# Input projection in the order of its waiters, and layer 1's modulation between the expert slots of two sample blocks

## The reference

```python
m = silu(cond) @ w_ada + b_ada                  # w_ada (1024, 6144): the modulation, for c_ctx and for c
sh1, sc1, g1, sh2, sc2, g2 = split(m, 6)
h = rmsnorm(x, norm1_g) * (1 + sc1) + sh1
proj = h @ w_in                                 # c_q, c_kv, k_pe | z | xbc | dt | glu
mix = concat(attention, ssd(z, xbc, dt), conv_module(glu)) @ w_out
x = x + g1 * mix
h = rmsnorm(x, norm2_g) * (1 + sc2) + sh2
q = h @ peer_wq                                 # 8 heads, top 16 of 128 x 128 keys: 128 experts a token
x = x + g2 * sum_k gate_k * gelu(u[idx_k] . h) * v[idx_k]
```

## Time and profile before

| | |
|---|---|
| median of 3 runs | 5076.69 us (5076.66 to 5082.86) |
| profiled execution | 5067.13 us |
| its span | 5065.3 us, mean TensorE clock 0.918 |
| PE, DVE, ACT, POOL busy | 3905.9, 3247.4, 743.5, 1442.1 us |
| gathers (software queue) | 1342.26 MB, 66.2% of 16 engines |
| direct loads | 153.13 MB, 9.4% |

### The profile page before, as it was taken

One profiled execution on the slowest core, in us unless ns is written; L12 is line 12 of the kernel. 1 busy time (PEld: TensorE's weight loads), 2 busy tenths in 40 slices (PEclk: granted clock), 3 DMA queues, 4 the chain that ended last, 5 costly groups with the idle time before them and its releaser, 6 DMA issues. The chain is left out here.

```text
span 5065.3 us, 36421 instructions
## 1 busy us (share of the span) xinstructions
PE 3905.9 (77%) x11046; PEld 1925.4 (38%) x11046; DVE 3247.4 (64%) x8263; ACT 743.5 (15%) x2205; POOL 1442.1 (28%) x1284
## 2 busy tenths in 40 slices
PE   7479577889777777778868776789987777777776
PEld 6365233554223222235535632346432322222222
DVE  1534866644887867854474648664468787687666
ACT  0121124311101001010022111341111100100101
POOL 0001122211444444432222011222134444344432
PEclk9689688999998999999989887899999999999999
DMA  8244346763998998999959334567469999899998
GB/s 262 71 131 142 140 174 225 260 220 128 404 418 362 421 421 365 421 395 390 371 205 355 135 125 159 205 237 259 156 252 421 388 401 421 366 421 421 415 421 343
DMA packets 342149, 1497.72 MB, mean 296 GB/s; under 512 B 31424, under 2 KB 176448, under 8 KB 178112
## 3 DMA queue, kind: packets, MB, share of 16 engines
q0 software_dynamic: 184320, 1342.26, 66.2%
q1 hardware_dynamic: 157632, 153.13, 9.4%
HBM read 1491.97 MB, written 3.31 MB: 295 GB/s over the span
## 5 line engine op out<-in xcount | busy, mean ns | idle before, releaser
L650 PE MATMUL expert_acc<-uv_ring,diag 128*128 128x512 f32 x3744 | 1895.4, 640 | 430.1 <-DVE diag L1207 420.7
L604 POOL DMA_INDIRECT uv_ring<-uv,expert_index x936 | 1051.9, 1124 | 2816.8 <-PE expert_acc L650 2249.1
L650 PEld LDWEIGHTS expert_acc<-uv_ring,diag 128*128 128x128 f32 x3744 | 702.1, 201 | 1515.1 <-DVE diag L1207 898.2
L1198 DVE CUSTOM_DVE_ANT_0 uv_ring<-uv_ring,arena 128x1024 f32<-128x1024 f32 x680 | 832.0, 1224 | 236.9 <-DMA uv_ring<-uv,expert_index 234.1
L650 PE MATMUL expert_acc<-arena,diag 128*128 128x512 f32 x1376 | 692.4, 636 | 258.1 <-DVE diag L1207 189.8
L1207 DVE TENSOR_SCALAR diag<-const_mats,expert_gate,gelu 128x128 f32<-128x128 f32 x1280 | 465.4, 364 | 372.9 <-ACT gelu L929 276.4
L929 ACT ACTIVATE gelu<-u_dot 128x1 f32<-128x1 f32 x1280 | 256.3, 203 | 2995.9 <-DVE u_dot L1198 2991.9
L604 POOL DMA_INDIRECT arena<-uv,expert_index x344 | 390.0, 1134 | 763.6 <-PE expert_acc L650 465.2
L1198 DVE CUSTOM_DVE_ANT_0 arena<-arena 128x1024 f32<-128x1024 f32 x344 | 420.9, 1224 | 174.1 <-DMA arena<-uv,expert_index 172.4
L650 PEld LDWEIGHTS expert_acc<-arena,diag 128*128 128x128 f32 x1376 | 248.6, 197 | 692.9 <-DVE diag L1207 403.4
L1198 DVE CUSTOM_DVE_ANT_0 uv_ring<-uv_ring,prompt_rows 128x1024 f32<-128x1024 f32 x256 | 312.2, 1220 | 86.8 <-DMA uv_ring<-uv,expert_index 86.1
(11 more groups left out here) (201 smaller groups left out, 2788.3 us busy)
## 6 DMA issues: line engine op xcount, KB each, us to landing
w_ring<-w_ada SPq DMA_DIRECT2D x66, 512.0 KB
w_ring<-w_in SPq DMA_DIRECT2D x64, 512.0 KB
w_ring<-w_pq SPq DMA_DIRECT2D x64, 512.0 KB
w_ring<-w_out SPq DMA_DIRECT2D x32, 512.0 KB
uv_ring<-w_ada SPq DMA_DIRECT2D x30, 512.0 KB, 6.0
uv_ring<-uv,expert_index POOLq DMA_INDIRECT x936
arena<-b_ada SPq DMA_DIRECT2D x48, 128.0 KB
arena<-uv,expert_index POOLq DMA_INDIRECT x344
```

Source lines behind the costliest of these rows:

```text
L604: pool.indirect_dma_start(out=UV[j], out_offset=None, in_=uv, in_offset=bass.IndirectOffsetOnAxis(ap=idxs[:, n % 2, k:k + 1], axis=0)).the ...
L650: ins = pe.matmul(acc[:, half, :], diag[:, m % DIAGS, :], UV[SLOT_AT[m]][:, D + 512 * half:D + 512 * half + 512], start=(k == 0), stop=(k ...
L1198: V_.tensor_tensor_reduce(UV[j][:, 0:D], UV[j][:, 0:D], rows_of(n), 1.0, 0.0, ALU.mult, ALU.add, dots[:, m % DOTS:m % DOTS + 1]).then_inc( ...
```

## The change

1. **Input projection.** px comes directly behind pa, each xt as soon as its silu can be there, then pg, and pz last: four tiles ahead of the taps on PE (two on ACT), the rest between the taps; DVE makes a gate of z after every third tap. On PE cs and cb now stand behind the taps' points, and DVE makes gm behind the taps. Units of w_in are loaded in the new order. The same in all four mixers.
2. **Modulation.** b_ada comes by one DMA as 24 rows of 256; a ninth product of each unit adds the row (a column of the identity, spread, times the rows). ACT drains the tiles instead of DVE. Layer 0's runs at the start as before, with the three layer-weight loads now behind its weights; ACT norms the prompt behind it.
3. **Layer 1's modulation** stands in the slots of sample blocks 2 and 3 of layer 0 (b = 1 and 2): one unit behind `add_v` and `gelu` of slots 5, 15, ..., 115, through `w_ring` alone. Silu(cond) is made at the start of block 2.
4. **Block 4** runs beside the prompt mixer alone; `BESIDE_PROMPT` has 138 advances for the 131 that a block needs, 52 of them ahead of the taps.
5. Small things: the product in `add_peer` is written in place in PSUM, iota and some scratch tiles are moved.

```diff
+def mod_unit_at(l, b, k):
+    return (b - 1) * ADA_UNITS // 2 + k // 10 if l + 1 < L and b in (1, 2) and k % 10 == 5 and k < 5 * ADA_UNITS else None

-BESIDE_PROMPT = points(("mod", range(24), 2), ("n1", [1], 3), ("pa", range(2), 2), ("pz", range(2), 2), ("px", range(6), 1),
-                       ("pg", range(4), 1), ("conv", [5], 2), ("taps", range(4, 30, 5), 1), ("cT", [0], 2), ("st", range(2), 3),
-                       ("yT", [0], 2), ("v", [0], 2), ("head", range(6), 2), ("wo", range(4), 2), ("n2", [1], 3),
-                       ("pq", range(16), 1))
+BESIDE_PROMPT = points(("n1", [1], 8), ("pa", range(2), 5), ("pz", range(2), 3), ("px", range(6), 3), ("pg", range(4), 3),
+                       ("conv", [5], 4), ("taps", range(4, 30, 5), 3), ("cT", [0], 4), ("st", range(2), 5), ("yT", [0], 4),
+                       ("v", [0], 4), ("head", range(6), 2), ("wo", range(4), 2), ("n2", [1], 4), ("pq", range(16), 1))

+def in_tiles(g):
+    nb = GROUP_BLOCKS[g]
+    return ([("pa", i) for i in range(2 * nb)]
+            + [("px", 0), ("px", 1), ("px", 2), ("xt", 0), ("px", 3), ("xt", 1), ("px", 4), ("xt", 2), ("px", 5), ("xt", 3),
+               ("pg", 0), ("xt", 4), ("pg", 1), ("pg", 2), ("pg", 3)])
+def with_taps(g, ahead):
+    n = 2 * GROUP_BLOCKS[g]
+    out = [("pz", i) for i in range(min(ahead, n))]
+    for k in range(CMK):
+        if k % 3 == 2 and ahead + k // 3 < n:
+            out.append(("pz", ahead + k // 3))
+        out.append(("taps", k))
+    return out
+POINTS_AT = {("xt", 0): [("px", 0)], ("xt", 1): [("px", 1)], ("xt", 2): [("px", 2)], ("xt", 3): [("px", 3)], ("xt", 4): [("px", 4)],
+             ("pg", 1): [("px", 5), ("pg", 0)], ("pg", 2): [("pg", 1)], ("pg", 3): [("pg", 2), ("pg", 3), ("conv", 5)]}
...
 # sync
+                sp.dma_start(bada[0:ADA_UNITS, :], b_ada[l].rearrange("(u n) -> u n", n=WU)).then_inc(s_brow.sem, 16)
+                for u in range(ADA_UNITS):
+                    load_w(w_unit(l, 0, "ada", u), w_ada[l, :, u * WU:(u + 1) * WU])
...
 # tensor: a unit (MOD_GROUPS[u]: unit u's product, then the transposes of the row before it)
+                        for c in range(DC):
+                            pe.matmul(t[:, 0:WU], hT[:, c, 0:P], w[:, c, :], start=(c == 0), stop=False)
+                        ins = pe.matmul(t[:, 0:WU], C[0:ADA_UNITS, C_ID, u:u + 1].broadcast_to([ADA_UNITS, P]), bada[0:ADA_UNITS, :],
+                                        start=False, stop=True)
...
                         for k in range(SLOTS):
                             add_v(n, k)
+                            unit = mod_unit_at(l, b, k)
+                            if unit is not None:
+                                modulate(l + 1, unit)
...
 # scalar
                             gelu(n, k)
+                            unit = mod_unit_at(l, b, k)
+                            if unit is not None:
+                                modulate(l + 1, unit)
...
+                        if (s, i) == ("px", 1) or s == "xt":
+                            silu_tanh(0 if s == "px" else i + 1)
+                            beside.point("px", 0 if s == "px" else i + 1)
...
 # vector
+                            if k % 3 == 2 and k // 3 < 2 * nb:
+                                gate_z(k // 3)
                             beside.point("taps", k)
```

More of the change, by code:

```diff
@@ L209, in psum_order @@
     for l in range(L):
-        out += [(s, l, 0, i) for s, i, _ in mod_steps()]
+        if l == 0:
+            out += [(s, 0, 0, i) for s, i, _ in itertools.chain(*MOD_GROUPS)]
         for g in range(2):
@@ L686, in _ @@
                     pe.wait_ge(*free["n1"].at(l, g, 2 * nb - 1))
[L687 to L717, removed]
+                    for s, i in in_tiles(g) + with_taps(g, 4):
+                        if s == "taps":
+                            beside.point("taps", i)
+                            continue
+                        if s == "xt":
+                            pe.wait_ge(*s_silu.at(l, g, i))
+                            t = fill("xt", l, g, i)
+                            src = ctmp[i % 2] if i < 4 else BC[:, 0]
+                            for b in range(nb):
+                                ins = turn(t[:, b * P:(b + 1) * P], src[:, b * P:(b + 1) * P])
+                        else:
+                            u = in_unit(s, i, nb)
+                            w = weights(l, g, "in", u)
+                            t = fill(s, l, g, i)
+                            if s in ("px", "pg"):
+                                for c in range(DC):
+                                    ins = pe.matmul(t[:, 0:T], w[:, c, (i % 2) * P:(i % 2 + 1) * P], hT[:, c, 0:T],
+                                                    start=(c == 0), stop=(c == DC - 1))
+                            else:
+                                b, width = i % nb, WU if u != 1 else TOK - 256
+                                for c in range(DC):
+                                    ins = pe.matmul(t[:, 0:width], hT[:, c, b * P:(b + 1) * P], w[:, c, 0:width],
+                                                    start=(c == 0), stop=(c == DC - 1))
+                        done(ins, s)
+                        for stage, k in POINTS_AT.get((s, i), [(s, i)] if s in ("pa", "pz") else []):
+                            beside.point(stage, k)
@@ L730, in _ @@
                                        start=True, stop=True), "cb")
-                    for k in range(CMK):
-                        beside.point("taps", k)
                     pe.wait_ge(*s_glu.at(l, g))
@@ L1314, in _ @@
                             ins.then_inc(s_cconv.sem, 1)
-                        for s, i in {0: [("px", i) for i in range(3)], 1: [("px", i) for i in range(3, 6)] + [("pg", i) for i in range(4)]}.get(c, []):
-                            beside.point(s, i)
                         if c >= 1:
```

276 lines of the change are left out of this document (142 added, 134 removed).

## The result

The changed kernel takes 5043.24 us (median of 4 runs, 5030.11 to 5048.69) against 5078.03 (4 runs, 5076.66 to 5082.86) beside it on the same chip: ratio 0.9927, 95% interval 0.991 to 0.9943. In a second session it was 5038.76 (5037.54 to 5047.22), ratio 0.9926 (0.9907 to 0.9945). So it is faster, by 0.7%. I had forecast 4945, and 5020 as the top of the range.

A forecast was written before the change was run, and what follows sets the result against it. DMA was taken to bound expert blocks and layer 1's modulation, PE and DVE order the sample mixers; −3 − 20 − 32 + 70 − 115 − 32 = −132 gave 4935 profiled, 4945 us median, 8-in-10 range 4885 to 5020.

The forecast's parts named there:

- Start, −3: Layer 0's modulation at the start: DVE's b_ada hole goes, −11.9, bias products add +10.9; sum −3 us.
- Prompt mixer of layer 0, −20: Layer 0's prompt mixer: z tiles leave the front, transposes and conv run between x tiles; −20 us.
- Sample mixers, −32 each: Both layers' sample mixers: taps start at 504.5 against 553.8, less z gates and later masks; −32 us each.
- the bill behind the last tap: Sample mixers: cs and cb queue behind the last tap's slots, so DVE waits for masks and ct; +13.4 us.
- Blocks 2 and 3, +70: Layer 0's sample blocks with the modulation units: +60 for DMA bytes, +5 a block for engine stops; +70 us.
- Layer 1's prompt mixer, −115: Stage from block 3's end, block 4 beside it: DMA-bound at 2.53 us a transfer, 446 us against 562; −115.
- The rule on ACT's tables: Conv steps: alternating tanh and gelu load a table each change; 2.66 us by the skill page would add some 11 us.
- Rival C: Whole kernel: forecast with the dearer table change, total −121, 4956 us; chance 0.04.
- D: Layer 1's prompt mixer: five-buffer ring sets a slower slot pace, 4.49 us or more; +8 to +73; chances 0.05 and 0.08.
- A: Blocks 2 and 3: the units' stops are not absorbed, blocks +163, total −39, 5038 us; chance 0.13.
- B: Layer 1's prompt mixer packs better through idle PE, stage about 400 us, total −178, 4899 us; chance 0.12.

The follow-up runs named there:

- e17: The changed kernel again, unedited, in the second session: 5038.76 us, ratio 0.9926.
- e2: Changed kernel with PE's slots of each conv chunk put ahead of its wait for the silu and the xt transposition: 4999.14 us, ratio 0.9851.
- e28: Changed kernel with e2's edit and one slot a point, not three, beside conv chunks and gate tiles of layer 1's prompt mixer: 4997.01 us, ratio 0.9841.
- e11: Changed kernel with all 128 slots of block 4 ahead of layer 1's prompt mixer, none beside it: 5058.34 us, ratio 0.9973.
- e15: Changed kernel with one slot a point beside the conv chunks, ring of four not five, four modulation units loaded ahead not five: 5227.26 us, one run.

## Why the prediction was wrong, step by step

*Start, −3.* Measured +0.8 (first pa tile 137.46, now 138.28). The hole behind the second unit is gone, as these rows of PE show, but the bias product costs more than I took:

```profile
25.72 0.69 PE L708 MATMUL rotating<-b_ada_rows,const_mats 24*128 24x256 f32 x2
26.34 3.72 PE L707 MATMUL rotating<-w_ring,hT 128*128 128x256 f32 x16
29.99 0.69 PE L708 MATMUL rotating<-b_ada_rows,const_mats 24*128 24x256 f32 x2
```

0.69 us for two, where I had 0.45 from sixteen in a run.

*Prompt mixer of layer 0, −20.* Measured −19 (sample transposes from 344.6 to 326.3, with the start's +0.8). *Sample mixers, −32 each.* Measured −30 and −24 (in e17's profile the second is −37). Taps at 485.8 (I had 504.5 less the 23 us of the earlier steps, 481.5), and the bill behind the last tap came as forecast:

```profile
554.62 0.76 DVE L1415 TENSOR_TENSOR arena<-rotating,const_mats 128x256 f32<-128x256 f32 x2 [4.13 <-PE rotating L769]
557.61 0.76 DVE L1415 TENSOR_TENSOR arena<-rotating,const_mats 128x256 f32<-128x256 f32 x2 [2.23 <-PE rotating L769]
```

*Blocks 2 and 3, +70.* Measured +69.4, DMA share 1.01. The number was right, its make-up only half: I added 60 for bytes and 10 for stops, and the runs show two limits, each near the whole cost by itself (+69 for the bytes, +53 for the stops), so that the sum came out is in part luck.

*Layer 1's prompt mixer, −115: the step that failed.* Measured −16.4 (567.6 to 551.2). In the words of the step: "52 + 9 units, less 3 prefetched units and 4 or 5 prefetched slots, is 54 × 2.53 = 137". With the 12 us before them that put the taps 149 us behind block 3; they came at 228.0, 79 us late. The other 20 us that are missing lie behind the first tap: the taps took 75 us, not 62, and from ct to yT it was 71.5, not 62.

Of the 79 us, 43 are the lock step, which the prediction didn't have: with e2's edit the taps come at 184.6. The other 36 are the price of a slot. 2.53 us was from a row with 21 slots and 9 weight units in 76.4 us, two queues side by side, and I called that row DMA-bound. Its stretch in the trace of before:

```profile
2464.00:2541.00 77.00, 71.20 (x313) 45.64 (x311) 38.23 (x89) 8.34 (x37) 20.99 (x20) 0.98 0.93 349
```

PE is busy 71 of 77 us there, as full as DMA at 0.93. Counted in slots alone the row says 3.64 us, and 12 + 47.5 × 3.64 = 185 is what e2 shows. This agreement is with one run and no law: e28, with 20 slots fewer there, needs 122.4 where the same price gives 112. Alone in the ring of five a slot took 2.84 us (e11), and with one buffer fewer and the same bytes the stage grew by 80 (e15), so the ring counts, not the bytes alone. Even with e2's edit the stage's DMA share is 0.81. How the 36, and the 20 behind the first tap, are shared between the ring and the mixer's own chain I didn't pull apart.

*The steps together.* +0.8 − 19 − 30 + 69.4 − 16.4 − 24 = −19, and the spans of the two profiles differ by 18.4.

*The rule on ACT's tables* fell with its premise. I wrote that tanh and gelu in turn load a table at each change. ACT's timeline of after, in the conv chunk and at dt's exponential behind it:

```profile
2369.75 0.20 ACT L970 ACTIVATE gelu<-u_dot 128x1 f32<-128x1 f32 x1 [3.10 <-DVE u_dot L1269]
2369.86 0.26 ACT L1050 ACTIVATE arena<-rotating 128x128 f32<-128x128 f32 x1
2372.55 0.28 ACT L1052 ACTIVATE arena<-rotating 128x128 f32<-128x128 f32 x1 [2.44 <-PE rotating L669]
2372.73 0.30 ACT L1031 ACTIVATE arena<-arena 128x128 f32<-128x128 f32 x1
...
2498.93 1.28 ACT L1042 ACT_TABLE_LOAD   x1
2500.22 0.21 ACT L1042 ACTIVATE dt<-dt 128x16 f32<-128x16 f32 x1
```

Between the gelu and the tanh (L1031) there is no load, nor any from 2350 to 2498; the whole kernel has 154 against 148 before. In all of it no load stands between a gelu and the next tanh (30 places), and none between a tanh and the next gelu in 29 of 37; in the other 8 an exponential or a logarithm had come just before the tanh. So loads go with exponentials and logarithms: at them, or at what follows. A load is 1.28 us, and in 99 of the 154 the function follows within 20 ns. So the drain of 1.38 us that the Trainium skill, ScalarE: Activation LUTs, What ACT_TABLE_LOAD costs, adds doesn't show here. The sum isn't touched: I had costed these loads at nothing. Rival C falls with the rule.

*The rivals.* D named the failing step: "a burst of 8 or 10 slots outruns" the ring, and "every further slot waits a full round". It had the bursts at the wrong place: the points of three beside the conv chunks did it, as PE's slots stood behind a wait for DVE. I gave D 0.13 together, priced at 4.49 us a slot and more; block 4 came to 508.4 / 128 = 3.97. Its argument against, that the modulation kept 377 GB/s with the same five buffers, held for slots with weight loads between them, which don't use the ring. A (blocks +163) and B (a better packed mixer) are refuted by the table. That A's total, 5038, lies 5 us from the measured median is chance: its blocks cost 69 and not 163, and the mixer's missing 99 us make up for that.

## What to carry to other kernels

Price work that goes through a ring by its own count in the nearest rows, never by all transfers of that stretch: other queues' bytes ride along and make the pace look better than the ring can give. Before work is moved out of a stretch, see whether its engines were full there (DMA 1.03, PE 171 of 172): then it was cover for what stays, and in another full stretch it can cost more (here 75.6 us, not 50.5). When two engines' slots are tied to points of another chain, put the slots that free buffers ahead of any wait for the engine that waits for those buffers.

## What the runs showed of the hardware

In the lock step TensorE's granted clock was 0.80 in the mean of 2341 to 2470, so part of the stretch at the lower of its levels, 1.2 GHz and not 2.4, and it was busy 0.59 of it. In e2's stretch it was 0.94, busy 0.78; twelve matmuls there took 5.32 us, and 7.01 at 2352.65 above. So the stalls may have cost some clock too; no run separates this from the lock step:

```profile
2342.00:2459.00 117.00, 91.07 (x301) 47.59 (x300) 63.23 (x147) 14.85 (x59) 34.99 (x35) 0.94 0.94 351
```

```profile
2367.12 5.32 PE L689 MATMUL expert_acc<-uv_ring,diag 128*128 128x512 f32 x12
```

The same kernel's profiled runs differ by 11 us (5046.9 and 5035.7 of span), nearly all of it in layer 1's sample mixer (after block 4, 832.9 and 821.8 us to block 5's end), so differences of 10 us between single profiles of whole kernels say nothing; the stages of the table repeat within 4 us.
